# Stick-breaking jobs: the older block's values between its successor's first and second turned group, and the products beside the later groups

## The reference, cut to what matters

```python
z = einsum(q_blk, k) * scale                       # scores, 128 queries x up to 1024 keys
log_1mb = where(strict, log_sigmoid(-z), 0)
between = cumsum(log_1mb, reverse=True) - log_1mb
a = where(strict, exp(log_sigmoid(z) + between), 0)
out = einsum(a, v)
```

## Time and profile before

| | us |
|---|---|
| median of 3 runs | 2693.02 (2692.38 to 2693.81) |
| the profiled execution | 2691.86 |
| its span, first to last instruction | 2690.1 |
| TensorE busy | 2603.7 (97% of the span) |
| stick-breaking steps in the trace (step 0 to the end of step 32) | 49.99 to 324.87 |
| one job of eight steps (job 2, steps 16 to 23) | 181.70 to 247.92 |

### The profile page before, as it was taken

One profiled execution on the slowest core, in us unless ns is written; L12 is line 12 of the kernel. 1 busy time (PEld: TensorE's weight loads), 2 busy tenths in 40 slices (PEclk: granted clock), 3 DMA queues, 4 the chain that ended last, 5 costly groups with the idle time before them and its releaser, 6 DMA issues.

```text
span 2690.1 us, 39379 instructions
## 1 busy us (share of the span) xinstructions
PE 2603.7 (97%) x12614; PEld 2081.1 (77%) x12614; DVE 1865.2 (69%) x2575; ACT 1053.6 (39%) x2143; POOL 1829.9 (68%) x1403
## 2 busy tenths in 40 slices
PE   7999999999999999999999999999999999999998
PEld 5777777677778888887777788877887888888887
DVE  6666687728888888887786465674458576666667
ACT  5544455535534333433443233564234322222212
POOL 4555532457698888886779984322468898888874
PEclk9999999999999999999999999999999999999999
DMA  4322232034211111124443435313443111111134
GB/s 151 106 87 87 87 95 71 16 126 152 76 59 55 55 55 55 55 63 164 142 128 106 120 104 191 106 57 116 168 130 133 48 59 56 55 55 55 55 129 142
DMA packets 98697, 253.55 MB, mean 94 GB/s; under 512 B 9423, under 2 KB 13296, under 8 KB 98292
## 3 DMA queue, kind: packets, MB, share of 16 engines
q1 hardware_dynamic: 72464, 186.41, 22.5%
q10 hardware_dynamic: 26084, 65.21, 6.7%
HBM read 211.20 MB, written 37.77 MB: 93 GB/s over the span
## 4 chain that ended last, share of the span: by engine, by line
PE 78%; DVE 7%; POOL 6%; ACT 4%; issue 3%; DMA 1%; POOLq 0%; ACTq 0%; DVEq 0%; SPq 0%
PE ps L1283 9%; PE ps L1285 9%; PE ps L1284 9%; PE ps L1668 7%; PE ps L1669 7%; PE ps L1670 7%; PE ps L1715 4%; PE ps L1717 4%; PE ps L1716 4%; PE ps L1374 2%; PE ps L1390 2%; PE ps L1899 2%; PE ps L1901 2%; PE ps L1900 2%; PE ps L1405 1%
## 5 line engine op out<-in xcount | busy, mean ns | idle before, releaser
L944 POOL CAST wh<-raw 128x1024 fp32r<-128x1024 f32 x139 | 150.9, 1086 | 467.4 <-PE ps L1285 411.9
L1283 PE MATMUL ps<-hh,wh 128*128 128x512 f32 x1040 | 434.7, 418 | 20.2 <-DVE hl L3344 11.8
L1285 PE MATMUL ps<-hh,wl 128*128 128x512 f32 x1040 | 409.5, 394 | 0.0
L1284 PE MATMUL ps<-hl,wh 128*128 128x512 f32 x1040 | 408.7, 393 | 0.0
L946 POOL TENSOR_TENSOR wl<-raw,wh 128x1024 fp32r<-128x1024 f32 x139 | 337.5, 2428 | 11.1
L1074 POOL TENSOR_TENSOR wl<-raw,wh 128x512 fp32r<-128x512 f32 x156 | 212.4, 1376 | 71.8 <-ACT wh L2537 70.7
L1283 PEld LDWEIGHTS ps<-hh,wh 128*128 128x128 f32 x1040 | 197.0, 189 | 73.4 <-issue 14.0
L1285 PEld LDWEIGHTS ps<-hh,wl 128*128 128x128 f32 x1040 | 196.5, 189 | 43.5
L1284 PEld LDWEIGHTS ps<-hl,wh 128*128 128x128 f32 x1040 | 197.3, 190 | 34.8 <-issue 2.4
L3740 DVE TENSOR_TENSOR hlf<-ps,hlf 128x512 f32<-128x512 f32 x252 | 171.5, 691 | 23.9 <-PE ps L1717 21.7
L1669 PE MATMUL ps<-al,wh 128*128 128x512 f32 x476 | 185.2, 389 | 0.0
(11 more groups left out here) (486 smaller groups left out, 7222.5 us busy)
## 6 DMA issues: line engine op xcount, KB each, us to landing
raw<-weights SPq DMA_DIRECT2D x149, 512.0 KB, 3.7
raw<-weights SPq DMA_DIRECT2D x240, 256.0 KB, 2.6
arena<-w_ada SPq DMA_DIRECT2D x48, 512.0 KB, 3.8
arena<-gate_scratch ACTq DMA_DIRECT2D x25, 512.0 KB, 5.2
gate_scratch<-arena ACTq DMA_DIRECT2D x14, 512.0 KB, 2.6
gate_scratch<-sums_f ACTq DMA_DIRECT2D x17, 256.0 KB, 2.0
arena<-x_t ACTq DMA_DIRECT2D x1, 4096.0 KB, 14.1
x_scratch<-arena ACTq DMA_DIRECT2D x2, 2048.0 KB, 9.3
```

What stands on the lines that cost most here:

```text
L1283: pe.matmul(out, wh[:, slot, w], xh, start=start, stop=False)
L1284: pe.matmul(out, wh[:, slot, w], xl, start=False, stop=False)
L1285: return pe.matmul(out, wl[:, slot, w], xh, start=False, stop=stop)
```

## The change

Two things, both in TensorE's loop over the steps. The values of stick-breaking pairs lose their place ahead of the turned groups and go where those of the differential pairs are: behind the first group and ahead of the second. And in the stick-breaking steps that turn four groups and have values, no product goes between the first and the second group, so that the six come as three times two, behind the second, third and fourth.

```diff
                 if s < A_N:
                     a_scores(s)
-                beside = s in VALUES_AT and VALUES_AT[s] < SB_N
-                if beside:
-                    a_values(VALUES_AT[s])
                 if turning:
                     ahead = min(left, 3 if s == 1 or s % NB == 0 and s < SB_N else 2 if s > SB_N else 0)
                     fill(ahead)
                     left -= ahead
                     a_turn(TURN_AT[s], *turning[0])
-                if s in VALUES_AT and not beside:
+                if s in VALUES_AT:
                     a_values(VALUES_AT[s])
...
                 for n, turn in enumerate(turning[1:]):
-                    count = min(left, -(-left // (len(turning) - n)))
+                    between = s < SB_N and s in VALUES_AT and n == 0 and len(turning) > 2
+                    count = 0 if between else min(left, -(-left // (len(turning) - n)))
                     fill(count)
                     left -= count
                     a_turn(TURN_AT[s], *turn)
```

## The result

| | before, us | changed, us |
|---|---|---|
| median | 2693.02 (5 runs, 2692.38 to 2693.89) | 2706.37 (5 runs, 2699.72 to 2706.89) |
| ratio to before, 95% | | 1.0047 (1.0036 to 1.0058) |
| the profiled execution, its span | 2691.86, 2690.1 | 2706.89, 2705.1 |
| mean granted clock of TensorE there | 0.995 | 0.992 |
| steps 2 to 32, scores of 2 to scores of 33 | 257.82 | 273.65 |

A forecast was written before the change was run, and what follows sets the result against it. TensorE, busy 97%, was taken as the bound. Odd steps 3.2, job 0 0.4, even steps 2.3 and wide blocks 2.0 us gave 7.9, rounded 8.0: profiled 2699.9, median 2701.0 us, range 2696.5 to 2704.0.

The forecast's parts named there:

- The sum of waits and switches: All terms over the stick-breaking steps together: 7.9 us slower, 8.0 with roundings.
- Odd steps, the bare trip: Odd steps such as 19: TensorE waits for bank 4's copy behind the first group, 1.44 us trip, +0.32 us.
- Steps 21 and 23: ScalarE's two sigmoids come ahead of the copy, so the second group starts at 1.60 and 1.82: +0.24 us each.
- Even steps, the entry into values: Values behind a turned group cost one more change between full array and halves: 0.18 us a step, 2.3 in all.
- Job 0: Steps 2 to 7 of the first job, where ScalarE is delayed further: +1.74 us together.
- the bias rows: In job 0 they delay ScalarE further, moving step 5's second group from 1.60 to 1.93; 0.4 us with step 7.
- Steps 8 and 9 and their like: First group of a wide block, steps 9, 17, 25: values lose their cover behind the `v_out` wait, +0.67 us each, 2.0 together.
- Does it stay?: Whether step 17's first group still starts at 193.40: yes, as GpSimd makes no way during VectorE's scan, despite starting earlier.
- The second rival: GpSimd's earlier `s_weigh` in steps 8, 16, 24 brings `v_out` earlier: only 3.8 us slower, 2696.8; chance 0.12.
- A free entry: Only scores pay for the array change, not values: 5.1 us slower, 2698.1; chance counted within the forecast's 0.82.
- the third: Values cover the first trip in odd steps, 4.8 us less; with GpSimd's earlier finish about 2692, no slower; chance 0.03.
- three runs of two products: In steps with four groups the order gives these, not two runs of three; either would cost the same.

The follow-up runs named there:

- e4: The changed kernel with the modulation's one-column matmuls moved two steps later, to steps 12, 20 and 28: 2701.88 us, ratio 1.0033.
- e1: The changed kernel with the old count of products, so that only the values move: 2704.45 us, ratio 1.0044.
- e12: The changed kernel with the modulation's one-column matmuls moved four steps later, to steps 14, 22 and 30: 2699.46 us, ratio 1.0025.
- e9: The kernel before with only the values moved behind the first group in steps 9, 17 and 25, no product moved: 2699.90 us, ratio 1.0024.
- e2: The kernel before with only the new count of products, values ahead of the first group as they were: 2705.08 us, ratio 1.0049.
- e6: The changed kernel with VectorE's `v_out` ahead of `mod_add` in steps 8, 16 and 24: 2698.70 us, ratio 1.0022.
- e8: e7 with `v_out` ahead of `mod_add` as in e6, and the changed order in steps 9, 17 and 25 alone: 2688.85 us, ratio 0.9985.
- e10: The changed kernel with two products ahead of the first group in steps 9, 17 and 25: 2700.35 us, ratio 1.0026.
- e3: The changed kernel with the values ahead of the first group again in steps 9, 17 and 25: 2700.51 us, ratio 1.0026.
- e11: e8 with the modulation's one-column matmuls in steps 12, 20 and 28, as in e4: 2685.79 us, ratio 0.9973.
- e7: The kernel before with products two, two, two and none in ten odd steps that turn four groups: 2689.64 us, ratio 0.9990.
- e5: The changed kernel once more, unaltered, for a second profile: 2706.86 us, ratio 1.0051.

## Why the prediction was right or wrong

**The sum of waits and switches was right.** It was 7.9, and the two kernels with all of the change and a full clock show 8.4. Term by term:

- *Odd steps, the bare trip:* +0.32 forecast for step 19, +0.32 in e4. The trips of 1.44, 1.60 and 1.82 were 1.43 (step 19), 1.60 (step 13: 164.87 to 166.47) and 1.81 (step 15: 180.60 to 182.41). The rows of step 13, in the changed kernel:

```profile
164.87 0.66 PE L1390 MATMUL ps<-mats,arena 128*128 128x128 f32 x4
165.45 0.66 PE L1405 MATMUL ps<-arena 128*64 128x128 f32 x8
166.47 0.41 PE L1390 MATMUL ps<-mats,arena 128*128 128x128 f32 x2 [0.36 <-ACT arena L2396]
```

- *Steps 21 and 23:* +0.24 each forecast, +0.26 each.
- *Even steps, the entry into values:* 0.18 taken between 0 and 0.3; 0.16 to 0.24 measured in e1 and in the changed kernel. The row that was missing is there now: in step 16 the values start 0.52 behind a group of four, 0.16 more than a product does (0.36):

```profile
191.46 0.60 PE L1390 MATMUL ps<-mats,arena 128*128 128x128 f32 x4
191.98 1.31 PE L1405 MATMUL ps<-arena 128*64 128x128 f32 x20
```

  The Trainium skill, TensorEngine Tiling (Array Packing), Key Properties, has TensorE drained at each change of the tiling mode; e1's 0.2 in every even step agrees. It is a net price: scores (64*128 in the rows) and values (128*64) are two different halves, and the change between them that the old order had is gone, while values now have the full array ahead of them as well as behind. So where the prediction counted one more change between the full array and halves, there are two more, and one between the halves less.
- *Job 0:* 1.74 forecast, 1.85 to 1.88 measured. Step 5 came as forecast (+0.54 against 0.24 and the 0.33 of the bias rows), step 7 too (+0.36 against 0.34). Step 4 was underrated (+0.42 in place of 0.18), step 6 a little (+0.26 in place of 0.18), and step 3 overrated (+0.13 in place of 0.32).
- *Steps 8 and 9 and their like:* +0.67 forecast, +0.64 in e4 (0.22 and 0.42). The first group of steps 9, 17 and 25 starts 11.72 behind the scores of the step before in all three jobs, against 11.70.

**"Does it stay?" was answered rightly, for the reason given.** In the changed kernel `s_weigh` did start early, and ran on for 3.58 us instead of 2.31. The timeline of all engines and that of GpSimd:

```profile
193.21 2.26 DVE L3561 TENSOR_TENSOR_SCAN arena<-arena,reset 128x1024 f32<-128x1024 f32 x1
195.40 2.95 DVE L3517 SCALAR_TENSOR_TENSOR arena<-arena,cols 128x1024 f32<-128x1024 f32 x1
198.27 0.68 DVE L3532 COPY arena<-ps 128x512 f32<-128x512 f32 x1
```

```profile
193.68 3.58 POOL L975 TENSOR_TENSOR arena<-arena 128x1023 f32<-128x1023 f32 x1 [2.54 <-ACT arena L2390]
```

The scan ends at 195.47, GpSimd at 197.26, 1.79 later; in the earlier trace rows it was 1.80. Starting 1.27 us earlier against the scan gained it nothing. The Trainium skill, SBUF — State Buffer, Who interferes with whom, tells of an exclusive lock on the shared port pair, and this row agrees with it more sharply than those before. The second rival fails here, where it could have been right: `v_out` ends no earlier.

**The rivals.** A free entry (2698.1) is refuted by e1, the second rival by the row just read, and the third, that the values cover the trip, by the twelve waits for L2396. That there would be three runs of two products was right.

**The step that failed is that the sum took TensorE's clock as full throughout.** "The profiled execution would take 2699.9": all terms were waits and switches at the clock of the kernel before, 1.00 in every step from 2 to 32. No term asked what a longer wait, with the modulation's small matmuls not far off, does to it. So the step that was wrong is a term put at nothing, and it measured 7.6 us in the profile, and 5 to 6 by the medians below. The account of the profiled executions: spans differ by 15.0. Steps 2 to 32 hold 15.8 of it, made of 8.26 for waits and switches and 7.58 for five falls (1.23, 1.64, 1.49, 1.63 and 1.59, each as the step's excess over the same or a like step without a fall). Step 1, whose order did not change, is 0.51 longer. On the other side, before's fall in the steps that follow is missing:

```profile
340.60:344.00 3.40, 3.40 (x12) 2.76 (x12) 3.30 (x8) 0.73 (x3) 1.11 (x1) 0.51 0.53 154
```

This is the kernel before; the changed kernel's same step is 1.55 shorter (7.35 in place of 8.90). 15.8 + 0.5 - 1.5 = 14.8, and 0.2 are the net of the rest, in which the profile of before has five falls and that of the changed kernel six, at partly different places.

The runs without a profile tell the same by their mean clock. In the changed kernel the run at 0.996 took 2699.72 and those at 0.992 2706.89 and 2706.67; the other two are at 0.993. Its fastest run ended in the range, and so did the medians of e4 and e12, which have its waits. And the medians tell it by their size. Take the falls out of the column of steps 2 to 32, so that the waits at full clock are left, and subtract that from the difference of the medians: 5.1 and 5.8 us remain for the changed kernel (five and six falls), 4.2 for e9 (three), 1.8 to 2.5 for e1, e2, e6, e8 and e10 (one or two), and -1.0 to 0.1 for e3, e4, e11 and e12 (none). Only e7 (-0.1 with one fall) does not fit. The upper end of 2704.0 had room for a dearer entry and for GpSimd's work, but none for the clock.

**What brings the falls is partly open.** Counted by steps over the fourteen profiles:

| steps | with | falls |
|---|---|---|
| 9, 17, 25 | wait of 1.5 to 1.7 us, modulation in 10, 18, 26 (changed twice, e1, e9) | 7 of 12 |
| 9, 17, 25 | the same wait, modulation elsewhere (e4, e12) | 0 of 6 |
| 9, 17, 25 | wait of 0.7 us or less (the other eight) | 0 of 24 |
| 11, 19, 27 | the long wait two steps earlier, modulation directly ahead (changed twice, e1, e9) | 9 of 12 |
| 11, 19, 27 | no long wait, modulation directly ahead (before, e2, e3, e6, e7, e8, e10) | 5 of 21 |
| 11, 19, 27 | modulation elsewhere (e4, e11, e12) | 0 of 9 |

The seven of the first row begin 0.3 to 1.2 us behind the end of the wait. By these counts the long wait takes part in both kinds, and the modulation in the falls right behind it. That the modulation takes part in the first kind as well is not shown: it can't explain a fall in step 9 (e5, e9), where none of it has run yet, and why e4 and e12 have none in their six steps with the full wait stays open. One execution of each kernel was profiled (two of the changed one), and the count has luck in it. Steps 33 and 35, which no kernel changes, have a fall in six and in nine of the fourteen profiles; step 35 stands directly behind the last of this modulation. Outside steps 2 to 32 every profile has five to nine stretches at half speed, its last microseconds not counted. Step 1, also unchanged, takes 0.02 to 0.51 us more than before in the profiles without a fall in it, so the half us there is no effect of the change that can be shown; and e12's 2.4 us below e4 are in part the 1.3 between the kernels before beside them, and the rest lies within their intervals.

The Trainium skill, TensorE: Matmul & The Clock Gate, A second HAM failure mode: psum-queue depth-cycling, describes another kernel (bf16), in which frequent short idle moments between groups of matmuls, with the PSUM banks cycled, let the clock go down and up between its two levels. This kernel agrees in part: no wait of TensorE in steps 2 to 32 of the changed kernel is longer than 1.6 us, the clock moves between its two levels, and waits for PSUM bank 4 are what was added. But e4 and e12 have the same waits and no fall there, and at 148.6 the clock fell behind 3.60 us in which the rows show TensorE busy throughout.

## What to carry to other kernels

A reordering on an engine that is 97% busy is to be priced twice: by its waits at full clock, and by what they may do to the clock, at 1.2 to 1.6 us a fall here; a range that has only the first is too narrow on the slow side. A step's windows with the granted clock, read beside the distance between starts, separate the two in one look. Where one buffer goes round (bank 4 here), the group and what stands behind it must together be longer than the round trip, 1.44 us at the least here: with two products they take 1.71 to 1.83, with one product (an estimated 1.14) or the values of a narrow block (about 1.0) they do not reach it.

## What the runs showed of the hardware

- The clock of TensorE went to half for 3.4 us at a time, at 1.2 to 1.6 us of cost each, once or more inside a steady loop of steps that TensorE fills to over 95%. The kernel before has six such falls in its whole profile, all behind step 32, besides its last microseconds. Over the 73 of its runs beside e1 to e12, 0.001 of mean clock goes with about 1.9 us, in a spread from 2684 to 2698.
- The falls of steps 11, 19 and 27 come 1.0 to 2.2 us behind the end of the one-column matmuls, though the rows show these as 1.84 us of busy TensorE. With them moved, e4, e11 and e12 show none there, nor where they were moved to, in one profile each.
- The falls of steps 9, 17 and 25 come 0.3 to 1.2 us behind the end of a wait of 1.5 to 1.7 us, in 7 of the 18 steps that have such a wait, and in none of the 24 that have not.
- Transposes on the full array followed by values on half of it start 0.52 us apart, against 0.36 with a product behind them; a step with this one change more takes 0.16 to 0.25 us longer (e1).
- A 1023-wide product on GpSimd ends 1.8 us after the scan on VectorE, whether it started 0.5 or 1.8 us before the scan's end (2.31 and 3.58 us long).
